# Feed-forwards as seven block products in place of eight, their down part after all gates; experts' turns on the whole array; attention masks by a bf16 product

## What is computed

```python
def swiglu_ffn(x, g, w_gate, w_up, w_down):
    h = rmsnorm(x, g)
    return (jax.nn.silu(h @ w_gate) * (h @ w_up)) @ w_down       # D_FF = 2816, five times

for i in range(DEPTH):                                           # first stack, DEPTH = 2
    x = x + 0.5 * swiglu_ffn(x, ffn1_norm[i], ...)
    h = rmsnorm(x, mix_norm[i])
    x = x + (even_mixer(h, ...) if i % 2 == 0 else odd_mixer(h, ...))
    x = x + 0.5 * swiglu_ffn(x, ffn2_norm[i], ...)

def masked_softmax(s, mask):                                     # in the mixers, s scaled by 64 ** -0.5
    s = jnp.where(mask, s.astype(jnp.float32), NEG_INF)
    return jnp.where(mask, jax.nn.softmax(s, axis=-1), 0.0)

def expert_block(args):                                          # top 2 of 8 experts for each token
    xb, e = args
    return (jax.nn.silu(xb @ w_gate[e]) * (xb @ w_up[e])) @ w_down[e]
```

## Time and profile before

| | us |
|---|---|
| median of 3 runs | 3458.57 (3447.68 to 3472.22) |
| profiled execution | 3458.2 |
| its span (first to last instruction) | 3456.4 |
| TensorE busy | 3355.3 (97%) |
| VectorE busy | 777.2 (22%) |
| ScalarE busy | 508.1 (15%) |
| granted TensorE clock, mean | 0.98 |

### The profile page before, as it was taken

The page is one execution under the profiler, slowest core; times in us unless marked ns, Lnnn a source line. Parts: engine busy times, 40 slices in busy tenths (PEclk is TensorE's granted clock), DMA queues, the critical chain, the costliest instruction groups (busy, mean ns, idle before and its releaser), DMA issues. The chain is left out here.

```text
span 3456.4 us, 49430 instructions
## 1 busy us (share of the span) xinstructions
PE 3355.3 (97%) x21749; PEld 2009.6 (58%) x21749; DVE 777.2 (22%) x1562; ACT 508.1 (15%) x1168; POOL 169.8 (5%) x157
## 2 busy tenths in 40 slices
PE   8999999999999999999999999899999999999999
PEld 6765677777557767677467667675433333333333
DVE  1013400100240013533200025623212112121122
ACT  1012400100130013313010033222200000000000
POOL 0000000000000000311001012200100000000000
PEclk9999999999999999979999999989999999999999
DMA  7332044343224333103253331124399999899993
GB/s 301 146 134 105 6 181 161 133 164 137 98 86 189 146 137 126 61 7 148 110 204 146 122 143 49 62 75 168 150 381 390 394 392 392 346 390 392 388 396 149
DMA packets 73846, 665.66 MB, mean 193 GB/s; under 512 B 9728, under 2 KB 10368, under 8 KB 13344
## 3 DMA queue, kind: packets, MB, share of 16 engines
q1 hardware_dynamic: 69120, 651.26, 47.7%
q10 hardware_dynamic: 4512, 11.24, 0.9%
HBM read 661.42 MB, written 1.05 MB: 192 GB/s over the span
## 5 line engine op out<-in xcount | busy, mean ns | idle before, releaser
L662 PE MATMUL psum<-xT_norm,ring 128*128 128x256 f32 x3520 | 772.4, 380 | 0.0
L662 PEld LDWEIGHTS psum<-xT_norm,ring 128*128 128x128 f32 x3520 | 671.5, 191 | 113.0 <-issue 23.9
L3679 PE MATMUL psum<-ring,arena 128*32 128x512 f32 x5376 | 587.2, 592 | 0.0
L3679 PEld LDWEIGHTS psum<-ring,arena 128*32 128x32 f32 x5376 | 175.6, 110 | 383.9 <-issue 383.1
L673 PE MATMUL psum<-ring,arena 128*128 128x512 f32 x880 | 386.6, 592 | 0.0
L3713 PE MATMUL psum<-ring,arena 128*32 128x512 f32 x2688 | 293.6, 592 | 0.8 <-DVE arena L3845 0.8
L721 DVE TENSOR_TENSOR arena<-arena,psum 128x256 f32<-128x256 f32 x110 | 46.4, 421 | 1063.5 <-ACT arena L702 1063.5
L673 PEld LDWEIGHTS psum<-ring,arena 128*128 128x128 f32 x880 | 167.2, 190 | 187.0 <-issue 184.2
L3713 PEld LDWEIGHTS psum<-ring,arena 128*32 128x32 f32 x2688 | 88.7, 110 | 200.0 <-issue 190.7
L702 ACT ACTIVATE arena<-psum 128x256 f32<-128x256 f32 x110 | 42.3, 384 | 1034.1 <-PE psum L662 1034.1
L2582 PE MATMUL psum<-xT_norm,ring 128*128 128x256 f32 x832 | 184.2, 380 | 2.7 <-ACT xT_norm L550 2.7
(11 more groups left out here) (545 smaller groups left out, 2883.0 us busy)
## 6 DMA issues: line engine op xcount, KB each, us to landing
ring<-in_moe_w SPq DMA_DIRECT2D x340, 1024.0 KB, 7.2
ring<-in_ffn_w SPq DMA_DIRECT2D x50, 3072.0 KB, 10.0
ring<-in_merge_w SPq DMA_DIRECT2D x16, 2048.0 KB, 8.5
ring<-in_feat_w SPq DMA_DIRECT2D x12, 2048.0 KB, 8.4
ring<-in_ffn_w SPq DMA_DIRECT2D x15, 1024.0 KB, 9.7
ring<-in_ev_in_w SPq DMA_DIRECT2D x4, 2048.0 KB, 7.7
ring<-in_od_in_w SPq DMA_DIRECT2D x4, 2048.0 KB, 7.9
ring<-in_merge_w SPq DMA_DIRECT2D x8, 1024.0 KB, 11.5
```

Of the source, the lines that this page charges most:

```text
L662: last = pe.matmul(prog.psum[:, t, m * S:(m + 1) * S], wm[:, k, t * P:(t + 1) * P], prog.xT[:, k, :], start=(k == 0), stop=(k == KT - 1))
L3679: last = pe.matmul(psum[part(j), r, :], xg[:, u.i, u.group // GROUPS, r * P + BLOCK * j:r * P + BLOCK * (j + 1)], m[:, j, :], start=(u.i = ...
```

## The change

**Feed-forward.** A chunk is again 256 hidden columns. Tokens (two halves), the 1024 inputs (two halves) and the pair gate | up (two blocks of 256) make a 2x2 by 2x2 product of blocks, done with seven products of half depth (P1 to P7, four matmuls of 256 columns each) of mixed blocks: four mixes of x (once), four differences of weights for each chunk on VectorE, written to the ring, and seven sums on VectorE that give gate, up and hidden. Activations are now the stationary side, so hidden comes out by tokens and is turned by four transposes. All eleven chunks of gate-up go first; hidden and its four mixes stay in SBUF; then down runs as seven products a pair of 128-row blocks (one matmul of 512 columns each), added up in seven banks over the eleven pairs. Gate-up weights are 2 MB transfers, down weights 1 MB. `TURN_BANK` takes the turns, and the side's products come in halves.

**Experts.** `turn` transposes each round's 128x128 at once, six a group.

**Attention.** Queries are scaled by -1/8 when they are copied (`fill`); for the causal groups a bf16 identity times a bf16 mask opens each of the two score banks, the scores are added to it, the least and the exponentials read PSUM. Idle products are gone. `hide_all` holds bf16.

```diff
+def ffn_weights(prog, stream, first, total, layout):
+
+    slots, sums = FFN_LAYOUTS[layout]
+    pieces = [(stream[first][:, m * UNIT:(m + 1) * UNIT], slots[0] + m * UNIT) for m in range(2)]
+    pieces += [(stream[first + c][:, 0:2 * UNIT], slots[c % 3]) for c in range(1, total)]
+    free = [slots[i] + m * UNIT for i in ((total - 3) % 3, (total - 2) % 3) for m in range(2)]
+    pieces += [(stream[first + g][:, 2 * UNIT:3 * UNIT], free[g % 4]) for g in range(total)]
+    w = Weights(prog, pieces)
+    w.slots, w.sums, w.down = slots, sums, total + 1
...
+PRODUCTS = ("P1", "P6", "P5", "P7", "P2", "P4", "P3")
+FIRST_PRODUCTS = ("P1", "P2", "P5", "P6", "P7", "P4", "P3")
+LAST_PRODUCTS = ("P1", "P6", "P5", "P7", "P4", "P3", "P2")
+UP_BANK = {"P1": 0, "P2": 0, "P6": 1, "P5": 2, "P3": 2, "P7": 3, "P4": 4}
+DOWN_BANK = {"P1": 0, "P6": 1, "P5": 5, "P7": 3, "P2": 6, "P4": 4, "P3": 2}
+TURN_BANK = 7
+SUM_OF = {"P5": 1, "P6": 2, "P7": 3, "P4": 4}
+MIX_OF = {"P5": 1, "P6": 2, "P7": 3, "P3": 4}
...
+                if i < weights.down:
+                    c = i - 1
+                    if c > 2:
+                        sp.wait_ge(made, 7 * (c - 2))
+                    weights.start(sp, i)
+                    if c == 5 and loads:
...
+                if g < 4:
+                    sp.wait_ge(made, 7 * (total - 2 + g // 2))
+                else:
+                    if g == 4:
+                        sp.wait_ge(made, 7 * total)
+                    if behind:
+                        w, n = behind.pop(0)
+                        w.start(sp, n)
+                    sp.wait_ge(pair_used, g - 3)
...
+            def gate_up(c, name):
+                left, right = factors[name]
+                a, w = x_of[left], gate_up_weights(c)[right]
+                if name == "P1":
+                    if c == 0:
+                        weights.wait(pe, 0)
+                    else:
+                        weights.wait(pe, c + 1)
+                    if c == 1:
+                        pe.wait_ge(first_posted, 1)
+                        pe.wait_ge(posted, posted_at(0, "u2"))
+                    elif c:
+                        pe.wait_ge(silu_ready, 2 * c - 1)
+                if name == "P5" and c:
+                    pe.wait_ge(posted, posted_at(c - 1, "up0"))
+                if name == "P2" and c:
+                    pe.wait_ge(p1_copied, c + 1)
+                    pe.wait_ge(posted, posted_at(c, "u2"))
+                if name == "P3":
+                    if c == 0:
+                        weights.wait(pe, 1)
+                    pe.wait_ge(posted, posted_at(c, "up1"))
+                if name in SUM_OF:
+                    pe.wait_ge(summed, 4 * c + SUM_OF[name])
+                if name in MIX_OF and c == 0:
+                    pe.wait_ge(x_mixed_done, MIX_OF[name])
...
+                    if c == 0 and name in ("P1", "P2"):
+                        head.wait_k(pe, k + (KT // 2 if name == "P2" else 0))
+                    last = pe.matmul(psum[:, bank, 0:GROUP], a[:, k, :], w[:, k, :], start=(fresh and k == 0),
+                                     stop=(k == KT // 2 - 1), skip_group_check=True)
+                last.then_inc(made, 1)
+
+            def turn(c):
+                pe.wait_ge(posted, posted_at(c, "hidden0"))
+                if c:
+                    pe.wait_ge(copied, c)
+                for t in range(2):
+                    for i in range(2):
+                        last = pe.transpose(psum[:, TURN_BANK, (2 * t + i) * P:(2 * t + i + 1) * P], up[:, i, t * P:(t + 1) * P],
+                                            prog.ident)
...
-                else:
-                    down(g, 1, False, True)
-                if side and g in (1, 2):
-                    side.on_tensor(pe, g - 1, 2)
+            for c in range(total):
+                for name in order_of(c):
+                    gate_up(c, name)
+                    if c and name == "P6":
+                        turn(c - 1)
+            for g in range(total - 2):
+                for n, name in enumerate(PRODUCTS):
+                    last = down(g, name)
+                    if g == 0 and n == 3:
+                        turn(total - 1)
+                last.then_inc(pair_used, 1)
...
+                if side and 1 <= g <= 4:
+                    side.half_on_tensor(pe, g - 1, TURN_BANK)
+            for name in LAST_PRODUCTS:
+                down(total - 2, name)
+                down(total - 1, name).then_inc(acc_made, 1)
...
+            for c in range(total):
+                act.wait_ge(made, made_at(c, "P1"))
+                act.activation(p1, psum[:, UP_BANK["P1"], 0:GROUP], ACT.Copy).then_inc(p1_copied, 1)
+                if c:
+                    copy_turned(c - 1)
+                    act.wait_ge(made, made_at(c, "P2"))
+                    act.activation(silu[:, 0, :], psum[:, UP_BANK["P2"], 0:GROUP], ACT.Silu).then_inc(silu_ready, 1)
+                else:
+                    act.wait_ge(first_posted, 1)
+                    act.activation(silu[:, 0, :], first_gate, ACT.Silu).then_inc(silu_ready, 1)
+                act.wait_ge(posted, posted_at(c, "gate1"))
+                act.activation(silu[:, 1, :], gate1, ACT.Silu).then_inc(silu_ready, 1)
+            copy_turned(total - 1)
...
+            def sum_up(c, i):
+                w = gate_up_weights(c)
+                out, a, b = (("T1", "12", "11"), ("T2", "22", "T1"), ("T3", "22", "12"), ("T4", "T2", "21"))[i]
...
+                elif i in (1, 3):
+                    dve.wait_ge(summed, 4 * c + i)
+                dve.tensor_tensor(w[out], w[a], w[b], ALU.subtract).then_inc(summed, 1)
...
+            def sums_behind(c, i):
+                if c < total - 1:
+                    sum_up(c + 1, i)
+                else:
+                    sum_down(0, i)
```

On VectorE, the chunks' loop and the down part; then attention, the experts and the build:

```diff
+            for c in range(total):
+                if c == 0:
+                    dve.wait_ge(made, made_at(0, "P2"))
+                    dve.wait_ge(p1_copied, 1)
+                    dve.tensor_tensor(first_gate, psum[:, 5, 0:GROUP], p1, ALU.add).then_inc(first_posted, 1)
+                sums_behind(c, 0)
+                sums_behind(c, 1)
+                dve.wait_ge(made, made_at(c, "P6"))
+                dve.wait_ge(p1_copied, c + 1)
+                dve.tensor_tensor(u2, p1, bank("P6"), ALU.add).then_inc(posted, 1)
+                sums_behind(c, 2)
+                if c:
+                    mix_hidden(c - 1)
+                sums_behind(c, 3)
+                dve.wait_ge(made, made_at(c, "P7"))
+                dve.wait_ge(posted, posted_at(c, "u2"))
+                dve.tensor_tensor(v, bank("P7"), u2, ALU.add).then_inc(posted, 1)
+                dve.wait_ge(posted, posted_at(c, "v"))
+                dve.tensor_tensor(up[:, 1, :], bank("P5"), v, ALU.add).then_inc(posted, 1)
+                dve.wait_ge(made, made_at(c, "P4"))
+                dve.tensor_tensor(gate1, v, bank("P4"), ALU.subtract).then_inc(posted, 1)
+                dve.wait_ge(silu_ready, 2 * c + 2)
+                dve.tensor_tensor(up[:, 1, :], silu[:, 1, :], up[:, 1, :], ALU.mult).then_inc(posted, 1)
+                dve.wait_ge(made, made_at(c, "P3"))
+                dve.tensor_tensor(up[:, 0, :], u2, bank("P3"), ALU.add).then_inc(posted, 1)
+                dve.wait_ge(posted, posted_at(c, "up0"))
+                dve.tensor_tensor(up[:, 0, :], silu[:, 0, :], up[:, 0, :], ALU.mult).then_inc(posted, 1)
+            for i in range(4):
+                sum_down(1, i)
+            mix_hidden(total - 1)
+            for g in range(2, total):
+                for i in range(4):
+                    sum_down(g, i)
+                if meanwhile and g == 3:
+                    meanwhile.on_vector(dve)
+                if side and g == 7:
                     side.mean_on_vector(dve)
...
-                    pe.wait_ge(shifted, shifts[i - 1])
+                    if groups[i - 2].mask is None:
+                        pe.wait_ge(shifted, shifts[i - 1])
+                    else:
+                        pe.wait_ge(probs, i - 1)
+                if g.mask is not None:
+                    for x in range(2):
+                        pe.matmul(psum[:, 2 * (i % 2) + x, :], identity, spread(g.mask.unsqueeze(1), g.half, g.n),
+                                  start=True, stop=False, skip_group_check=True)
                 for j in range(g.half):
                     for x in range(2):
...
-            def keep_busy(i):
-
-
-                pe.wait_ge(shifted, shifts[i])
-                for _ in range(IDLE_PRODUCTS):
-                    pe.matmul(psum[:, 2 * ((i + 1) % 2), :], zeros, spread(zeros.unsqueeze(1), 4, P), start=True, stop=True)
...
-                    dve.scalar_tensor_tensor(t, psum[:, bank:bank + 2, :].rearrange("p x (j n) -> p (x j) n", j=g.half),
-                                             -g.scale, spread_keys(g.hide, g.count, g.n), ALU.mult, ALU.add).then_inc(shifted, 1)
+                if g.mask is None:
```

(35 more changed lines are left out.)

314 lines of the change are left out of this document (197 added, 117 removed).

## The result

| | us |
|---|---|
| before, median of 4 runs beside it | 3461.49 |
| after, median of 4 runs | 3362.87 (3350.11 to 3369.12) |
| ratio | 0.9701, 95% interval 0.9675 to 0.9728 |
| profiled execution of after | 3363.99 |

The change takes 98.6 us off the median, 94.2 off the profiled execution (3458.2 before). The forecast was 3352, off by 11 us of the 106 it expected. First the page of the kernel after: the busy rows, and the slices of the granted clock.

The account below looks back on a forecast made before the run. TensorE, busy for 97% of the span, was taken as the bound. Feed-forwards 86.5, experts 10.9 and attention 10, less 1 for GpSimd's interference, gave 106.4 us off 3458.2: 3352 us, own range 3338 to 3368.

Parts of the forecast that it names:

- Product count and transposes: Feed-forwards: seven products for eight save 19.0 and 9.4 us, added transposes cost 4.9; net 23.5 us each, 117.5 for five.
- The first chunk: Each feed-forward's start: P3 waits 4.5 us for VectorE's queue, and the lower clock behind it costs 1.7; 31 us in all.
- The fifth feed-forward: Last feed-forward: GpSimd's embedding scaling slows VectorE's differences beside it, costing 1 us; about 218 us from first to last matmul.
- Experts' turns: Experts: six whole-array transposes take 0.92 us in place of 1.31, 28 times, a gain of 10.9 us.
- Rival (c): Experts held by their weight stream, attentions by scores to turn: both small gains gone, 3373 us; chance 0.14.
- Attention: Both attentions: idle products go, mask products come, VectorE loses a pass; TensorE's lost work is gained, 10 us in sum.
- The margin of VectorE: Steady feed-forward chunks: VectorE needs 9.0 us against TensorE's 12.5, with 3.5 us to spare, so TensorE never waits.
- rivals b: Feed-forwards: TensorE waits in every chunk for a semaphore 0.5 to 1.5 us late, +55 us, 3407; chance 0.12.
- (d): Feed-forwards: VectorE's differences are slow; gain gone at 2.4 us each, 3540 us at 2.74 each; chance 0.05.
- The prediction's own walk: One steady feed-forward chunk followed on both engines: up1 done at 8.4 us, two products before P3 needs it; no TensorE wait.

Follow-up runs that it names:

- the new order: After, with VectorE making the first chunk's mixes and up1 ahead of chunk 1's differences, the rest of those later: 3335.6 us, ratio 0.9637.
- the attentions alone: The kernel before with only the attention change (bf16 mask products, queries scaled in the copy, no idle products): 3466.75 us, ratio 1.0014.
- the doubled differences: After, with every difference of weight blocks in the feed-forwards made twice, one behind the other: 3551.26 us, 2.6% slower than before.

## Why the prediction came out as it did

**Product count and transposes (23.5 us a feed-forward): right.** Without the first chunk's trouble the first four stages are 204.3 to 205.0 us against 227.6 to 228.9 before, on average 23.6 less. The chunk of 12.5 us is 12.52, between the same VectorE instruction of two chunks.

**The first chunk (4.5 us of stall, 1.7 of clock): right in sum, shared out otherwise.** The start of P3 was put at 14.9 us after the first matmul and is at 14.62 in the third feed-forward; the waits are 3.3 to 4.2, mean 3.8, against bounds of 3.5 to 5.0. The clock's part is larger than the 1.7 taken: with the new order 30.9 us went, 6.2 each, so that 2.4 lie beside the wait. 6.2 were forecast, by luck to the tenth, as the one part was too large and the other too small. The rule read from the earlier trace rows, a pause of some us and then some us at 1.2 GHz, held at a pause that did not exist yet.

**The fifth feed-forward: right.** 219.0 against 218. GpSimd works there from 1863.24 to 1874.01. Of the five differences that start meanwhile, three took 1.46, 2.72 and 2.30 us, the others 0.69 and 0.68. One of them, beside GpSimd's instruction:

```profile
1868.87 5.14 POOL L4275 TENSOR_TENSOR arena<-arena 128x1024 f32<-128x1024 f32 x2
1869.08 2.72 DVE L880 TENSOR_TENSOR arena<-arena,ring 128x512 f32<-128x512 f32 x1
```

TensorE waited for them once, 0.6 us.

**Experts' turns (10.9 us): right.** 10.5 in the profiles. Timeline of TensorE around one turn, beside the earlier trace rows:

```profile
2496.49 5.33 PE L3935 MATMUL psum<-ring,arena 128*32 128x512 f32 x48
2501.76 0.87 PE L3948 MATMUL psum<-constants,arena 128*128 128x128 f32 x6
2502.56 1.50 PE L3935 MATMUL psum<-ring,arena 128*32 128x512 f32 x12
```

48 records of 0.107 us (3.00 / 28 by the earlier trace rows) fill 5.14 us from 2496.49; the next tiled product starts 0.93 us after that, against the 0.92 of the sum, of which 0.27 is going over and back. The Trainium skill says (TensorEngine Tiling, Key Properties) that a change of tiling mode drains TensorE; the trace agrees, and this is its price here. Rival (c)'s first half, that the stream holds the experts, is out.

**Attention (10 us): wrong, 0.3 in the profiles of before and after, and nothing in the time of this part alone (8.1 in its profile, ahead of longer chains).** The step that failed is "In the first attention TensorE is busy 58.6 of the 62.6, so what it loses is gained". It counted the idle products as work only. The size of the work was right: the kernel with the new order had 59.0 us with 6.8 us of low clock in it, which cost 3.4, so 55.6 at full clock against 55 forecast. But the idle products held the clock, as the run without them shows (+29 us, all of it in the attentions). In six profiles without them (after twice, the attentions alone, before without them, the new order, the doubled differences) the first attention had a low stretch each time, 6.8 to over 60 us long; in five with them in all steps it had one once, of 10.2 us, and in the one with them in the first six steps it had none. Both things were in the text, the clock among what would make it wrong, yet with no term and no chance of its own, while the same text had priced the clock behind a stall. In the first attention the low clock took 11.4 us (67.0 against 55.6). Both attentions together are 9.7 of the 12.2 us by which the profiled execution missed the sum (94.2 against 106.4); the chains, for which nothing was forecast, are 4.6 of it, and the feed-forwards gave back 1.8. The time still fell inside the range because this term was 10 of 106 us.

**The margin of VectorE (rivals b and d): no wait in any steady chunk, so both are out**, and differences stayed at 1.22 us. But the reason "3.5 us to spare on VectorE" was too kind. That is its idle time in a chunk, and only what lies between up1 and P3 is to spare. The prediction's own walk had it: up1 at 8.4 us, P4's end at 10.8. In after:

```profile
675.97 0.42 DVE L922 TENSOR_TENSOR arena<-psum,arena 128x256 f32<-128x256 f32 x1
678.96 0.42 DVE L924 TENSOR_TENSOR arena<-arena,psum 128x256 f32<-128x256 f32 x1 [2.57 <-PE psum L756]
```

Up1 ends at 676.39, P3 starts at 678.76, and VectorE rests for 2.57 us. The expectation of the doubled differences took 2.56 us for the ring's spare time; the 14.86 of a doubled chunk (12.53 + 4 x 1.25 - 2.67) bears that out. So (d) is mis-sized: at 2.48 us a difference its formula gives 8 x 1.25 + 10 x 1.5 = 25 a feed-forward, and the chip gave 36 to 39 in the first four. An estimate by the ring is that a difference slower by y costs 8y + 10(4y - 2.56): 34.9 at the 1.26 tried; the rest goes with low clock (in the third feed-forward, chunks of 15.5 to 16.2 us beside those of 14.86). It gives 98.6 / 5 = 19.7 us, all that the change saves spread over the feed-forwards, at y = 0.94. By this estimate the edge of (d) is some 2.2 us a difference, not 2.4.

**Open.** The low stretch of the first attention is one of 23.9 us in both profiles of after, 18.7 us into the stage, and two of 3.4 us, 4.1 and 14.4 us into it, in three other kernels with the same attention code and other work ahead of it. What decides between the two, no run tells. Nor do TensorE's waits in the stage order the cases: 4.0 us before, with the clock at 1.00; 4.8 with the attentions alone and 5.2 in after. The chains, whose code is the same everywhere, took 312.3 (before) to 330.7 us (the attentions alone) in twelve profiles, and 316.9 and 319.4 in the two of the changed kernel; they carry part of the spread between runs, and what sets their low stretches is not shown either.

## What to carry to other kernels

When a change takes work away from an engine that sometimes rests, ask first whether that work held its clock: price what is left at both clock levels, and if the lower one is dear, try filler in the steps that have pauses only (here enough in one profile, its gain likely and not shown). When work is added to a helper engine, follow the one value that the main engine needs next, round the loop, rather than summing the helper's busy time. And look at the first pass of such a loop by itself: it had no cover here, and giving the engine what is needed now ahead of what is needed next was worth 22 us.

## What the runs showed of the hardware that was not expected

- TensorE at 97% busy by the records still ran at 1.2 GHz for 23.9 us (23.14 of 23.90 in the first attention of after): once low, the clock did not rise for all that time although short matmuls followed almost without a pause. What stood ahead was 15.43 busy of 18.75 us.
- The low clock of the same attention code cost 3.4 us in three kernels and 12 in a fourth (half the length of the low stretches, 6.8 and 23.9 us). The kernels differ only ahead of that code or outside it, and in the two executions of the fourth it came at the same place.
- A wait of 3.3 to 4.2 us cost 2.4 us more in clock behind it. In the kernel with doubled differences, nine waits of 1.7 us on average and one of 9.3 in a stage went with a mean clock of 0.95 over it.
